# Attention with values held in the array, probabilities normalized on ScalarE, and transposes one tick later

## What is computed

```python
logits = einsum(q, k) * scale + bias         # masked
p = softmax(logits, axis=-1)                 # SWA: over the logits and a sink
o = einsum(p, v)
y = x + (silu(gate) * o) @ w_out             # MOBA: no gate here
```

## Time and profile before

| | |
|---|---|
| median of 3 runs | 2316.03 us (2315.71 to 2318.09) |
| the profiled execution, its own time | 2317.46 us |
| its span, first to last instruction | 2315.7 us |
| TensorE busy (matmul) | 2303.6 us |
| VectorE busy | 1511.6 us |
| ScalarE busy | 1191.6 us |
| granted TensorE clock, mean | 0.998 |
| attention of DSA, SWA, MOBA in the span | about 179 to 293, 447 to 665, 883 to 981 us |

### The profile page before, as it was taken

How to read it: one execution, slowest core, us unless ns; L and a number is a source line. 1 busy time by engine, 2 the same in 40 slices (tenths; PEclk the granted TensorE clock), 3 DMA queues, 4 the chain that set the end, 5 groups by cost and what they waited for, 6 DMA issues and landing times.

```text
span 2315.7 us, 38343 instructions
## 1 busy us (share of the span) xinstructions
PE 2303.6 (99%) x13836; PEld 2014.6 (87%) x13836; DVE 1511.6 (65%) x1841; ACT 1191.6 (51%) x1588; POOL 110.8 (5%) x92
## 2 busy tenths in 40 slices
PE   9999999999999999999999999999999999999998
PEld 8888898888898888888888888888888888888887
DVE  8677868777758555688756666667555555554655
ACT  6446744476654444457554544544543543544543
POOL 0004012000012000000000000012000000000000
PEclk9999999999999999999999999999999999999999
DMA  6554545455445554455555555555565555555564
GB/s 245 180 171 168 174 169 189 166 168 162 158 155 208 191 196 151 161 187 190 194 196 178 198 179 198 176 195 200 182 205 180 197 198 176 193 204 173 194 205 146
DMA packets 117092, 425.89 MB, mean 184 GB/s; under 512 B 13343, under 2 KB 13623, under 8 KB 116840
## 3 DMA queue, kind: packets, MB, share of 16 engines
q1 hardware_dynamic: 114048, 415.29, 52.7%
q0 software_dynamic: 2256, 8.48, 1.1%
q10 hardware_dynamic: 664, 0.39, 0.1%
HBM read 421.92 MB, written 2.18 MB: 183 GB/s over the span
## 4 chain that ended last, share of the span: by engine, by line
PE 96%; DVE 1%; DMA 1%; ACT 1%; issue 0%; SPq 0%; DVEq 0%; ACTq 0%
PE GP L465 47%; PE GP L474 25%; PE GP L489 15%; PE PT L574 1%; PE GP L422 1%; PE GP L424 1%; PE GP L423 1%; PE OP L430 1%; PE LOG L595 1%; DMA RAW<-w_dram 1%; DVE WL L1204 0%; DMA X<-x_dram 0%; PE LOG L649 0%; ACT WH L837 0%; DVE K L1532 0%
## 5 line engine op out<-in xcount | busy, mean ns | idle before, releaser
L1204 DVE TENSOR_TENSOR WL<-RAW,WH 128x1024 fp32r<-128x1024 f32 x784 | 939.7, 1240 | 658.8 <-PE GP L474 403.4
L837 ACT ACTIVATE WH<-RAW 128x1024 fp32r<-128x1024 f32 x784 | 815.6, 1056 | 559.0 <-PE GP L489 180.3
L465 PE MATMUL GP<-H,WH 128*128 128x512 f32 x4064 | 959.0, 392 | 0.2 <-ACT WH L837 0.2
L465 PEld LDWEIGHTS GP<-H,WH 128*128 128x128 f32 x4064 | 752.5, 188 | 156.1 <-issue 3.9
L474 PE MATMUL GP<-H,WL 128*128 128x256 f32 x4064 | 519.0, 284 | 0.0
L474 PEld LDWEIGHTS GP<-H,WL 128*128 128x128 f32 x4064 | 506.5, 192 | 13.1 <-issue 2.8
L489 PE MATMUL GP<-WH,G 128*128 128x512 f32 x1024 | 253.8, 389 | 0.0
L489 PEld LDWEIGHTS GP<-WH,G 128*128 128x128 f32 x1024 | 191.9, 188 | 39.7
L860 ACT ACTIVATE LO<-GP 128x512 f32<-128x512 f32 x151 | 89.4, 592 | 217.3 <-PE GP L474 217.1
L465 PE MATMUL GP<-G,WH 128*128 128x512 f32 x768 | 180.7, 390 | 0.0
L465 PEld LDWEIGHTS GP<-G,WH 128*128 128x128 f32 x768 | 142.0, 188 | 28.0
(11 more groups left out here) (248 smaller groups left out, 1372.2 us busy)
## 6 DMA issues: line engine op xcount, KB each, us to landing
RAW<-w_dram SPq DMA_DIRECT2D x784, 512.0 KB, 4.3
B<-bias_rows POOLq DMA_DIRECT2D x14, 512.0 KB, 5.2
X<-x_dram SPq DMA_DIRECT2D x4, 512.0 KB, 7.9
y_dram<-Y SPq DMA_DIRECT2D x4, 512.0 KB, 3.0
GAIN<-final_dram POOLq DMA_DIRECT2D x1, 1024.0 KB, 6.8
ONEHOT<-onehot_dram ACTq DMA_DIRECT2D x1, 148.5 KB
small<-small_dram ACTq DMA_DIRECT2D x1, 114.0 KB, 9.0
ident<-const_dram ACTq DMA_DIRECT2D x1, 64.0 KB
```

What stands on the lines that cost most here:

```text
L465: mm = pe.matmul(ps[:, n], wh[:, k, n * P:(n + 1) * P], R2[:, k0 + 4 * j + k], start=(j == 0 and k == 0), stop=False, skip_group_check=True)
L837: act.activation(WH[:, slot], RAW[:, slot], ACT.Copy).then_inc(hi_ready, 1)
L1204: dve.tensor_tensor(WL[:, slot], RAW[:, slot], WH[:, slot].bitcast(F32), ALU.subtract)\
```

## The change

- Probabilities times values has its operands swapped: the values of a head are stationary, the probabilities (transposed, as before) move, and OP holds features on the partitions and queries in the columns. For heads of 64 features one matmul takes two heads that share a half of the partitions: 64 stationary columns, 256 moving columns, two matmuls to a pack in place of eight. For MOBA's 128 features it is still eight of 128 moving columns. The packs are cut by key tile (4 heads of one kt) and not by head; their number stays.
- The transposes of o_sb and the pass that wrote it are gone; ScalarE copies OP straight to TF at the tick at which it copied PT.
- Row sums are inverted for each unit at d=4 on VectorE (one or two small instructions, no o_sb), and at d=5 ScalarE multiplies the four heads' probabilities by them in place: 4 copies with a scale, of 256 columns (qt=1) or 128.
- Transposes and pack copies go from d=5 to d=6, the products from d=6 to d=7. The flush counter starts a tick later and what hangs on it is due a number earlier, so gates and splits stay on their ticks.

```diff
@@ -159,8 +159,7 @@
 
     def packs(self, u):
 
-        blocks = [(h, kt) for h in range(4) for kt in range(self.units[u][1] + 1)]
-        return [blocks[k:k + 4] for k in range(0, len(blocks), 4)]
+        return [[(h, kt) for h in range(4)] for kt in range(self.units[u][1] + 1)]
 
     def n_banks(self, u):
         return sum(len(self.banks(v)) for v in range(u))
@@ -173,12 +172,12 @@
 
     def due(self, tick):
 
-        return [(u, tick - at, (tick - at - 6 - self.units[u][1]) if self.units[u][2] else None)
-                for u, at in enumerate(self.at) if 0 <= tick - at <= 13]
+        return [(u, tick - at, (tick - at - 7 - self.units[u][1]) if self.units[u][2] else None)
+                for u, at in enumerate(self.at) if 0 <= tick - at <= 14]
 
     def gate_at(self, u):
 
-        return {(SWA_HEADS, 5): 4, (SWA_HEADS, 9): 5}.get((self.heads, u), 3)
+        return {(SWA_HEADS, 5): 3, (SWA_HEADS, 9): 4}.get((self.heads, u), 2)
...
-                    if d - 5 in range(len(packs)):
-                        k = d - 5
-                        transposes([L[:, u % 2, h, kt * P:(kt + 1) * P] for h, kt in packs[k]],
-                                   (p_ready, u0 + u + 1), pt_ready, (pt_taken, pk + k + 1))
                     if d - 6 in range(len(packs)):
                         k = d - 6
+                        transposes([L[:, u % 2, h, kt * P:(kt + 1) * P] for h, kt in packs[k]],
+                                   (p_scaled, u0 + u + 1), pt_ready, (pt_taken, pk + k + 1))
+                    if d - 7 in range(len(packs)):
+                        k = d - 7
                         pe.wait_ge(pt_taken, pk + k + 1)
                         if k == 0 and chunk % a.per == 0 and fl:
-                            pe.wait_ge(o_ready, fl)
-                        for b, (h, kt) in enumerate(packs[k]):
-                            c = (4 * (chunk % a.per) + h) * a.hd
-                            mm = by_halves(OP[:, c:c + a.hd], pts[:, (pk + k) % 2, b * P:(b + 1) * P],
-                                           v_of(4 * chunk + h, kt), start=(c == 0 and kt == 0), stop=(kt == qt))
+                            pe.wait_ge(ot_taken, fl)
+
+                        p, first = pts[:, (pk + k) % 2, :], chunk % a.per == 0 and k == 0
+                        if a.hd == HD:
+
+                            c = 2 * P * (chunk % a.per)
+                            for m in range(2):
+                                mm = pe.matmul(OP[HD * m:HD * m + HD, c:c + 2 * P].rearrange("d (a q) -> d a q", a=2),
+                                               v_of(4 * chunk + m, k),
+                                               p.rearrange("k (a m q) -> k a m q", a=2, m=2)[:, :, m, :],
+                                               start=first, stop=(k == qt), skip_group_check=True)
+                        else:
+                            for h in range(4):
+                                mm = by_halves(OP[:, h * P:(h + 1) * P], v_of(4 * chunk + h, k),
+                                               p[:, h * P:(h + 1) * P], start=(first and h == 0), stop=(k == qt))
                         mm.then_inc(pv_done, 1)
-                    if flush == 2:
-                        transposes([o_sb[:, b * P:(b + 1) * P] for b in range(4)],
-                                   (o_ready, fl + 1), ot_ready, (ot_taken, fl + 1))
 
...
                        for u, d, flush in a.due(tick)]
                 for u, d, flush, chunk, qt, fl in due:
 
-                    if d - 5 in range(len(a.packs(u))):
-                        k = pk0 + a.n_packs(u) + d - 5
+                    if d - 6 in range(len(a.packs(u))):
...
                         act.wait_ge(pt_ready, k + 1)
...
-                    if flush == 2:
-                        act.wait_ge(ot_ready, fl + 1)
+
+                    if flush == 1:
+                        act.wait_ge(pv_done, pk0 + a.n_packs(u + 1))
                         if fl:
                             act.wait_ge(gl_ready, FLUSHED[fl - 1])
-                        act.activation(TF[:, :].rearrange("p (b q) -> p b q", b=4), PT[:, :, :],
-                                       ACT.Copy).then_inc(ot_taken, 1)
+                        act.activation(TF[:, :], OP[:, :], ACT.Copy).then_inc(ot_taken, 1)
                 for u, d, flush, chunk, qt, fl in due:
                     if d == 3:
                         nk = P * (qt + 1)
@@ -940,6 +946,14 @@
                                                  bias=neg_max[:, u % 4, h:h + 1],
                                                  accum_out=sums[:, fl % 2, c + h:c + h + 1])
                         ins.then_inc(p_ready, 1)
+                for u, d, flush, chunk, qt, fl in due:
+                    if d == 5:
+                        nk, c = P * (qt + 1), 4 * (chunk % a.per)
+                        act.wait_ge(sums_ready, u0 + u + 1)
+                        for h in range(4):
+                            ins = act.activation(L[:, u % 2, h, 0:nk], L[:, u % 2, h, 0:nk], ACT.Copy,
+                                                 scale=r_sums[:, c + h:c + h + 1])
+                        ins.then_inc(p_scaled, 1)
...
@@ -1348,20 +1362,13 @@
                         q = slice(qt * P, (qt + 1) * P)
                         g_lo(GL[:, t0:t0 + 4, q], tf, GH[:, t0:t0 + 4, q])
                 for u, d, flush, chunk, qt, fl in due:
-                    if flush == 0:
-                        n = 4 * a.per
+                    if d == 4:
+                        c = slice(4 * (chunk % a.per), 4 * (chunk % a.per) + 4)
                         dve.wait_ge(p_ready, u0 + u + 1)
                         if a is SWA:
-                            step(dve.tensor_tensor(sums[:, fl % 2, 0:n], sums[:, fl % 2, 0:n],
-                                                   sink_e[:, fl % 2, 0:n], ALU.add))
-                        step(dve.reciprocal(r_sums[:, 0:n], sums[:, fl % 2, 0:n]))
-                        dve.wait_ge(pv_done, pk0 + a.n_packs(u + 1))
-                        if fl:
-                            dve.wait_ge(ot_ready, fl)
-                        dve.tensor_tensor(o_sb[:, :].rearrange("p (h d) -> p h d", h=n),
-                                          OP[:, :].rearrange("p (h d) -> p h d", h=n),
-                                          r_sums[:, 0:n, None].to_broadcast([P, n, a.hd]), ALU.mult)\
-                           .then_inc(o_ready, 1)
+                            step(dve.tensor_tensor(sums[:, fl % 2, c], sums[:, fl % 2, c], sink_e[:, fl % 2, c],
+                                                   ALU.add))
+                        dve.reciprocal(r_sums[:, c], sums[:, fl % 2, c]).then_inc(sums_ready, 1)
                 for u, d, flush, chunk, qt, fl in due:
                     if gate is not None and flush == a.gate_at(u):
```

More of the change, by code:

```diff
@@ L374, in build @@
         pt_ready, pt_taken, pv_done = sem("pt_ready"), sem("pt_taken"), sem("pv_done")
-        o_ready, ot_ready, ot_taken, gated = sem("o_ready"), sem("ot_ready"), sem("ot_taken"), sem("gated")
+        sums_ready, p_scaled, ot_taken, gated = sem("sums_ready"), sem("p_scaled"), sem("ot_taken"), sem("gated")
         out_ready, out_done, last_squares = sem("out_ready"), sem("out_done"), sem("last_squares")
@@ L916, in attend @@
                 for u, d, flush, chunk, qt, fl in due:
-                    if d - 5 in range(len(a.packs(u))):
-                        k = pk0 + a.n_packs(u) + d - 5
+                    if d - 6 in range(len(a.packs(u))):
+                        k = pk0 + a.n_packs(u) + d - 6
                         act.wait_ge(pt_ready, k + 1)
```

## The result

The changed kernel took 2320.58 us (median of 19 runs, from 2317.06), the kernel before 2316.36 beside it (20 runs, 2315.57 to 2318.82): ratio 1.0015, interval 1.0008 to 1.0021. So it is slower by 3.5 us (1.8 to 4.9) by that ratio, by 4.2 between the medians, where 0.6 us faster was forecast: inside the predicted range, just inside what was called no change, but beyond what the runs leave open. A twentieth run of the changed kernel took 4609.2 us; it isn't explained and stays out.

A forecast was written before the change was run, and what follows sets the result against it. TensorE, busy 2303.6 of 2315.7 us, was taken to bound the kernel by its work and waits. -6.7 - 1.1 + 8.5 - 1.3 = -0.6 us, from 2316.03 to 2315.4; range for 8 in 10: 2309 to 2324.

The forecast's parts named there:

- Output transposes, -6.7: On TensorE, 16 groups of transposes of o_sb removed, 0.42 us each on average: -6.7 us.
- The product, -1.1: 64-feature heads' probabilities times values on TensorE: 0.76 us a pack against 0.79, -1.1 us for 36 packs.
- the third rival: Column halves don't overlap fully with different moving data: three slots for two, +7.6 us, 2323.0; four, 2331; chance 0.10.
- VectorE, 0: Reciprocals in place of flushes and the new d=4 wait for exps on VectorE: nothing, covered by its waits for TensorE.
- Rival 2: ScalarE reaches its ticks after the fourth weight copy 0.5 us later, as VectorE's d=4 wait delays loads: +7, 2322.5; chance 0.18.
- Scaled copies' stalls, +8.5: In attention, TensorE's transposes or sums wait for ScalarE's scaled copies in narrow places: +8.5 us, bounds 0 and 15.
- the two old waits, -1.3: TensorE's present attention waits, 0.7 us for exps and 0.6 for a pack copy, vanish as their steps move a tick.
- the 1.5 that was set aside for smaller places: Stalls at DSA tick 74, MOBA tick 25, two SWA places at position 1 and SWA tick 52: 1.5 us together.
- the five named places: Stalls at SWA tick 19 (2.2 us), DSA ticks 66 (1.2) and 70 (1.5), MOBA ticks 11 (1.5) and 18 (0.6).

The follow-up runs named there:

- the best kernel: Changed kernel with scaled copies at d=4 or d=3 for units starting at positions 0 or 1, SWA sums a tick later, second Silu at tick 67: 2308.94 us.

## Why the prediction was wrong

- **Output transposes, -6.7.** Right. Seven groups stand alone between big matmuls in the trace before and insert 0.42 to 0.44 us each; and without waits the whole saving shows.
- **The product, -1.1.** Right: 0.758 to 0.774 us a pack in place of 0.790 to 0.805, over the packs that stand alone between big matmuls and don't wait (18 and 11). 23.5 / 144 = 0.163 us to a record, somewhat over the 0.13 to 0.15 named, but not the 0.21 of the third rival, which falls. The rule of the Trainium skill that was set against it ("TensorE: Matmul & The Clock Gate", Part 3: matmuls start and end in program order) would give three slots, 0.97 us a pack; the measurement decides, and no record here shows a third slot.
- **VectorE, 0.** Right: the longest waits of TensorE for a weight copy, 0.3 and 0.7 us in the two profiles, stand at 23 us, ahead of the attention, where the kernel before waits 0.2; and the run without scaled copies and with the sums moved has VectorE's waits and keeps the whole saving. Rival 2's lag was there at two places, ScalarE reaching its ticks late by a landing, but not for rival 2's reason: those loads were issued before VectorE's wait at d=4.
- **Scaled copies' stalls, +8.5, with the two old waits, -1.3.** The failed step, by its size. The mechanism was right: ScalarE's order, the largest wait near 465 us, another near 900, 7.5 us in 6 waits for the scaled copies where 7 to 10 in 6 to 9 were named. But the two terms together were to cost 7.2 us, and cost 9.4 and 10.5 in the two profiles of the changed kernel: spans less 1.7 us for each 3.4 us at half clock, +1.6 and +2.7 against the kernel before, with the 7.8 us of saving put back. What was sized wrong: (1) SWA tick 19, 3.4 and 3.6 us for 2.2. ScalarE's next free moment was taken from the kernel before, where the weight pieces landed 0.4 and 0.6 us sooner; TensorE's arrival was right. (2) The product at DSA tick 67, 0.8 us, not named. The old wait in rows 6 didn't vanish as its step moved a tick, it moved along, since ScalarE's table load and Silu had only stood in front of another copy; so half of the -1.3 was wrong. (3) The sums of squares, 1.2 us in three places, took nearly all of the 1.5 that was set aside for smaller places, and the others took 0.4 more. (4) A wait costs some 0.2 us more than the list of waits has for it: 0.47 and 0.90 in the list at DSA ticks 66 and 70 are 0.7 and 1.1 from start to start. That the five named places sum to 7.3 us in the first profile, near the 7.0 forecast, is in part luck: singly they are off by -0.7 to +1.2, and in the second profile they make 8.7.
- **The granted clock, not in the sum at all.** Each long wait was priced at its length. Behind the one at SWA tick 19 a stretch at half clock follows in most executions and costs about 1.7 us more, and in some the clock falls behind shorter waits too. It makes the difference between some 1.5 to 2 us at equal clock and the 4.2 between medians, and the runs with one wait put back show it alone: beside the best kernel of their own batch (2309.69) 3.7 us for a wait of 3.2 us, 0.8 with matmuls in its place. The best kernel has 1.1 us of that wait left in one profile and none in the other. The Trainium skill says as much ("TensorE: Matmul & The Clock Gate", Part 1: the array's clock follows how busy it has been, and idleness halves it); the trace agrees, with 0.50 behind the wait in four profiles, and at 1.0 behind 3.15 us in one.
- **Where the gain went.** 7.8 us of saved TensorE work was there from the start; waits, 9.4 us more of them than before, took it and 1.6 more, and executions with more time at half clock the rest. It isn't inherent in normalizing on ScalarE: with the scaled copies placed by position and the sums moved along, the same work gives 9.0 and 7.5 us less than before in two batches. The scaled copies themselves are worth 2.5 us there (2308.94 against 2306.40).

## What to carry to other kernels

When steps of a schedule written out by hand move by a tick, list every other step that shares their buffer or bank and move it too: the sums of squares cost nothing before only because no transposes came in their tick. Place a new step of the off-bound engine where the bound engine will want its result, position by position, and not at a uniform distance. A step's free moment read from the kernel before holds only if what it waits for lands as it did there. Price a wait on TensorE of some microseconds at more than its length when the clock's records show a half-speed stretch behind it, in some executions if not in all; and compare runs at equal mean clock when effects are of a few microseconds.

## What was not expected of the hardware

- Behind a wait of 2.7 to 3.6 us TensorE's granted clock stood at 0.5 for 3.4 to 6.8 us in four profiles, and stayed at 1.0 behind one of 3.15 us in a fifth; in two it fell while the engine still stood (466.2 and 467.5, the transposes started at 467.5 and 468.0). 14 matmuls of no use in the wait's place kept it at 1.0 and made the kernel 1.9 and 2.9 us faster in two pairs.
- It also fell, in some executions, where small matmuls and short waits come together: behind the two-column sums of squares at 133 us (in the profiles of the kernel before and of four others), and behind waits of such sums, 0.77 us (at 435 us in one profile, at 591 and 596 in two) and 2.2 us (471 in one). Why in some executions and not in others stays open.
- Two matmuls with 64 stationary columns and different moving data, on the two column halves, insert 0.76 us with 256 moving columns each; as eight of 64 columns they insert 0.79. The number of matmuls hardly matters here. The columns do: eight of 128 columns (MOBA, before) take 1.02 us to the start of the next low matmul, eight of 64 take 0.61.
